# Where four 512 KB loads of the input are issued: SyncE's queue alone, or SyncE's and ScalarE's

## The chip, the cores and the metric

The kernel runs on one core of a Trainium2 chip, with that core's five engines (TensorE or PE, VectorE or DVE, ScalarE or ACT, GpSimd or POOL, SyncE or SP) and its 16 DMA engines. The metric is the device time of one execution in microseconds (us), lower is better, as the median of several runs.

## The reference

Two layers over an input x of 512 positions by 1024 channels, each with an adaLN modulation from a vector c. Cut to what the opening of the kernel works on:

```python
m = silu(c) @ w_mod + b_mod                       # shift, scale, gate
shift, scale, gate = jnp.split(m, 3, axis=-1)
h = rmsnorm(x, norm_g) * (1.0 + scale) + shift    # mean of x*x over 1024 channels
proj = h @ w_in                                   # layer 1: z, bg, cg, xh
y = shortconv_mixer(proj) @ w_out                 # layer 2: spatial gating mixer
x = x + gate * y
```

A final RMSNorm closes it. So nothing of the large products can start before the sum of x*x over all channels and the first columns of shift and scale exist.

## The kernel before

All arrays are transposed: channels on the 128 partitions, positions along the free dimension. x is eight tiles of 128x512 float32, `x_s`, loaded as four quarters of two tiles (512 KB each, 4 KB per partition). The weights come as one stream of slots of 512 KB. Products of full precision are made of three products of float32r, with each operand cut into a high part (ScalarE) and a low part (VectorE).

The opening goes like this. SyncE issues the four quarters of x (L367, semaphores `x_in[0]` to `x_in[3]`), then the stream in the fixed order `START_ORDER`: four slots of the modulation weights for the first channel pair (`raw_s`, "s0", L379), one weight slot (`raw`, L384), four slots "s1", two weight slots, then "s2", which waits until seven additions of the sum of squares are counted (`sq_added >= SQ_START`, with SQ_START 7), and so on. All of them go through one DMA queue, called q1 in the profile. ScalarE issues one load, `cols` (80 KB of constants, 640 bytes per partition, L601), on its own queue, q10; it then waits for it, makes silu(c) (L603) and squares the eight tiles of x in order, each pair after its quarter has landed (L606).

VectorE copies silu(c) into a wide tile `silu_w` (L1507), adds up the squares as they come (`ssum`, seven additions, L1512), takes a part of the modulation product (`acc_s`, L1421 and L1418) and then makes the variance. TensorE's program is in this order: six matmuls that serve only its clock (`keep_clock`, L1003), after the first square; `direct_columns(0, 0)`, 16 matmul instructions on the first slot of s0 (L1050); the column sums of `ssum`, after the seventh addition (L1063); `direct_columns(0, 1)` on the second slot (L1050); the sums of `acc_s` (L1040); the broadcast of the inverse root (L1034); then the first group of s1 (L1050) and the products themselves (L1077, L987 to L989). Engines execute their instructions in order.

The rest of the kernel, from about 54 us on, is two loops of products and two output projections; the changed lines are not in it.

Of the kernel before, what the change touches and what calls it, by code (L numbers as in the profile page):

```python
# [137 lines left out]
def build(nc, stream, xt, cols_d, wst_d, bs_d, out):  # L138
    ctx = ExitStack()
    with ctx:  # L140
# [3 lines left out]
        def sem(name):  # L144
            return ctx.enter_context(nc.semaphore(name))
# [5 lines left out]
        def at_kb(name, kb, shape, dt=F32):  # L151
            return nc.alloc_sbuf_tensor_at(name, shape, dt, offset=base + 1024 * kb)

        x_s = at_kb("x_s", 0, [P, KD, S])
# [84 lines left out]
        cols_in, x_in, ws_in, bs_in = sem("cols_in"), [sem(f"x_in{k}") for k in range(4)], sem("ws_in"), sem("bs_in")  # L239
# [123 lines left out]

        @block.sync
        def _(sp):
            for k in range(4):
                sp.dma_start(x_s[:, 2 * k:2 * k + 2, :], xt[:, 2 * k:2 * k + 2, :]).then_inc(x_in[k], 16)  # L367
            for q, what in enumerate(START_ORDER[:Q_RING]):
                if isinstance(what, str):
# [134 lines left out]
            for n in range(KD):  # L504
                half, k = n // DPAIRS, 2 * (n % DPAIRS)
# [53 lines left out]
        def _(act):  # L559
# [39 lines left out]


            act.dma_start(cols[:, :], cols_d[:, :]).then_inc(cols_in, 16)  # L601
            act.wait_ge(cols_in, 16)
            act.activation(silu_c[:, :], cols[:, C_C:C_C + KD], ACT.Silu).then_inc(sc_ready, 1)  # L603
            for k in range(KD):
# [1611 lines left out]
```

## Time and profile before

| | us |
|---|---|
| median of 3 runs | 821.37 |
| lowest and highest run | 821.09, 823.55 |
| the profiled execution, whole time | 824.04 |
| span of the profiled execution | 821.8 |

The page lists, for the profiled execution, the busy time of each engine, the span cut into 40 slices, the DMA queues, and the chain of work that ended last, followed back from the last instruction: at each step it goes to what released that step. A piece of that chain is time that sets the end; work that is not on it has slack. Between the span and the whole time of the profiled execution lie 2.24 us.

### The profile page before, as it was taken

The page shows a single profiled execution, that of the slowest core. Times are in us where ns is not written, and L with a number is a line of the kernel's source. Part 1 is how long each engine was busy: PE and PEld are TensorE (multiplying, and loading weights), DVE is VectorE, ACT ScalarE, POOL GpSimd, SP SyncE. Part 2 cuts the span into 40 slices and gives each one's busy share as a digit, 9 for nine tenths or more (in the row PEclk, how much of TensorE's full clock was granted, in tenths as well). Part 3 has the DMA queues.
Part 4 walks back from the last instruction along what each step waited for, and adds up shares of the span by engine and source line. Part 5 has one row for each costly group of instructions (what it writes and reads, how often), then busy time and mean ns, then how long its engine had stood idle before and what let it go on. Part 6 is the DMA issues. An engine that isn't in the chain of part 4 may idle for free.

```text
span 821.8 us, 15171 instructions
## 1 busy us (share of the span) xinstructions
PE 804.2 (98%) x5590; PEld 752.4 (92%) x5590; DVE 645.6 (79%) x942; ACT 438.5 (53%) x616; POOL 50.7 (6%) x64
## 2 busy tenths in 40 slices
PE   6999999999999999999999999999999999999996
PEld 6778999999999999987889888899999999988896
DVE  4989999999999999898553786657888888896534
ACT  3576665656656566553222854445676777752220
POOL 1010000000000000000000000010000000000000
PEclk9999999999999999999999999999999999999999
DMA  9885475656666656577421262405554454487103
GB/s 350 345 206 154 154 198 170 195 172 186 179 179 179 186 171 198 169 280 304 161 91 52 78 234 98 129 29 150 154 153 128 134 147 144 137 303 261 52 1 103
DMA packets 39501, 137.84 MB, mean 168 GB/s; under 512 B 4272, under 2 KB 6448, under 8 KB 39472
## 3 DMA queue, kind: packets, MB, share of 16 engines
q1 hardware_dynamic: 32128, 111.16, 36.9%
q0 software_dynamic: 6912, 25.17, 16.3%
q10 hardware_dynamic: 432, 1.13, 0.4%
q8 instruction: 17, 0.28, 0.1%
q14 instruction: 12, 0.10, 0.0%
HBM read 108.09 MB, written 4.19 MB: 137 GB/s over the span
## 4 chain that ended last, share of the span: by engine, by line
PE 93%; DVE 4%; DMA 1%; issue 1%; ACT 1%; SPq 0%; DVEq 0%; ACTq 0%
PE pp L1122 11%; PE pp L1123 11%; PE pp L1124 11%; PE pp L987 8%; PE pp L988 8%; PE pp L989 8%; PE p_aux L1122 7%; PE p_aux L1124 7%; PE p_aux L1123 7%; PE pp L1258 4%; PE pp L1259 4%; PE pp L1260 4%; PE p_aux L1332 2%; DVE acc_s L1418 1%; PE pp L1077 1%; DMA raw_s<-in_stream 1%
## 5 line engine op out<-in xcount | busy, mean ns | idle before, releaser
L1122 PE MATMUL pp<-h_hi,wh 128*128 128x256 f32 x280 | 79.3, 283 | 0.0
L1124 PE MATMUL pp<-h_hi,wl 128*128 128x256 f32 x280 | 79.2, 283 | 0.0
L1123 PE MATMUL pp<-h_lo,wh 128*128 128x256 f32 x280 | 79.2, 283 | 0.0
L1623 DVE TENSOR_TENSOR wl<-wt,wh 128x1024 fp32r<-128x1024 f32 x56 | 66.5, 1217 | 0.2 <-ACT wh L660 0.2
L660 ACT ACTIVATE wh<-wt 128x1024 fp32r<-128x1024 f32 x56 | 58.9, 1054 | 13.6 <-DVE wt L1604 7.6
L571 ACT ACTIVATE w_hi<-raw 128x1024 fp32r<-128x1024 f32 x29 | 30.6, 1058 | 61.8 <-PE pp L989 29.0
L1122 PE MATMUL pp<-s_hi,wh 128*128 128x256 f32 x224 | 63.4, 283 | 0.0
L1123 PE MATMUL pp<-s_lo,wh 128*128 128x256 f32 x224 | 63.4, 283 | 0.0
L1124 PE MATMUL p_aux<-s_hi,wl 128*128 128x256 f32 x224 | 63.4, 283 | 0.0
L1124 PE MATMUL pp<-s_hi,wl 128*128 128x256 f32 x224 | 63.4, 283 | 0.0
L1123 PE MATMUL p_aux<-s_lo,wh 128*128 128x256 f32 x224 | 63.4, 283 | 0.0
L1122 PE MATMUL p_aux<-s_hi,wh 128*128 128x256 f32 x224 | 63.4, 283 | 0.0
L987 PE MATMUL pp<-y_hi,w_hi 128*128 128x512 f32 (+1 forms) x160 | 58.5, 365 | 0.7 <-DVE y_lo L1684 0.4
L1397 DVE TENSOR_TENSOR w_lo<-raw,w_hi 128x1024 fp32r<-128x1024 f32 x32 | 38.9, 1222 | 22.8 <-ACT w_hi L571 22.3
L987 PE MATMUL pp<-y_hi,w_hi_b 128*128 128x512 f32 (+1 forms) x160 | 56.4, 353 | 0.0
L988 PE MATMUL pp<-y_lo,w_hi 128*128 128x512 f32 (+1 forms) x160 | 55.6, 348 | 0.0
L989 PE MATMUL pp<-y_hi,w_lo 128*128 128x512 f32 (+1 forms) x160 | 55.6, 347 | 0.0
L988 PE MATMUL pp<-y_lo,w_hi_b 128*128 128x512 f32 (+1 forms) x160 | 55.5, 347 | 0.0
L989 PE MATMUL pp<-y_hi,w_lo_b 128*128 128x512 f32 (+1 forms) x160 | 55.5, 347 | 0.0
L1122 PEld LDWEIGHTS pp<-h_hi,wh 128*128 128x128 f32 x280 | 53.7, 192 | 0.4 <-issue 0.4
L1123 PEld LDWEIGHTS pp<-h_lo,wh 128*128 128x128 f32 x280 | 53.8, 192 | 0.0
L1124 PEld LDWEIGHTS pp<-h_hi,wl 128*128 128x128 f32 x280 | 53.8, 192 | 0.0
(223 smaller groups left out, 2591.8 us busy)
## 6 DMA issues: line engine op xcount, KB each, us to landing
raw<-in_stream SPq DMA_DIRECT2D x144, 512.0 KB, 4.0
wl<-raw POOLq DMA_DIRECT2D x28, 512.0 KB, 4.5
raw_l<-in_stream SPq DMA_DIRECT2D x18, 512.0 KB, 5.5
raw_s<-in_stream SPq DMA_DIRECT2D x16, 512.0 KB, 13.3
wl_b<-raw POOLq DMA_DIRECT2D x16, 512.0 KB, 4.5
raw_m<-in_stream SPq DMA_DIRECT2D x14, 512.0 KB, 3.2
x_s<-in_xt SPq DMA_DIRECT2D x4, 512.0 KB, 6.0
w_lo_s<-raw POOLq DMA_DIRECT2D x4, 512.0 KB, 5.4
```

Of the source, the lines that this page charges most:

```text
L660: act.activation(wh[g % 2][:, at], wt[g % 2][:, at], ACT.Copy).then_inc(t_hi_cut, 1)
L987: pe.matmul(out, hi, rhs_hi(kt), start=first and n == 0, stop=False)
L988: pe.matmul(out, hi, rhs_lo(kt), start=False, stop=False)
L989: mm = pe.matmul(out, lo, rhs_hi(kt), start=False, stop=last and n == len(kts) - 1)
L1122: pe.matmul(out, hi, hi_of(k), start=fresh and k == 0, stop=False, skip_group_check=not fresh)
L1123: pe.matmul(out, hi, lo_of(k), start=False, stop=False, skip_group_check=not fresh)
L1124: mm = pe.matmul(out, lo, hi_of(k), start=False, stop=k == 3, skip_group_check=not fresh)
L1258: pe.matmul(v_bank(st)[:, :], left_hi, right_hi, start=kt == 0, stop=False)
L1259: pe.matmul(v_bank(st)[:, :], left_hi, right_lo, start=False, stop=False)
L1260: return pe.matmul(v_bank(st)[:, :], left_lo, right_hi, start=False, stop=kt == KD - 1)
L1397: dve.tensor_tensor(lo[:, slot[0], :], raw[:, slot[1], :], f32(hi[:, slot[0], :]), ALU.subtract).then_inc(consumed, 1)
L1623: dve.tensor_tensor(wl[par][:, part], wt[par][:, part], f32(wh[par][:, part]), ALU.subtract).then_inc(t_cut, 1)
```

## The change

Of the four quarters of x, SyncE issues only the first and the third. ScalarE issues the second and the fourth, right behind its load of the constants and ahead of its wait for them. The semaphores, the destinations and everything else stay as they are.

```diff
         @block.sync
         def _(sp):
-            for k in range(4):
+            for k in (0, 2):
                 sp.dma_start(x_s[:, 2 * k:2 * k + 2, :], xt[:, 2 * k:2 * k + 2, :]).then_inc(x_in[k], 16)
@@
             act.dma_start(cols[:, :], cols_d[:, :]).then_inc(cols_in, 16)
+            for k in (1, 3):
+                act.dma_start(x_s[:, 2 * k:2 * k + 2, :], xt[:, 2 * k:2 * k + 2, :]).then_inc(x_in[k], 16)
             act.wait_ge(cols_in, 16)
```

## Rows read from the trace of the kernel before

**Rows 1.** The page: busy time, and the chain that ended last, by engine.

```profile
PE 804.2 (98%) x5590; PEld 752.4 (92%) x5590; DVE 645.6 (79%) x942; ACT 438.5 (53%) x616; POOL 50.7 (6%) x64
PE 93%; DVE 4%; DMA 1%; issue 1%; ACT 1%; SPq 0%; DVEq 0%; ACTq 0%
```

**Rows 2.** The chain in order of time, first 30 us: start us, us, what.

```profile
0.75 0.39 SPq L367
...
2.13 0.50 SPq L367
...
2.67 8.07 DMA raw_s<-in_stream
10.74 0.14 issue
10.88 3.74 PE p_aux L1050 x16
14.62 1.51 PE p_aux L1063 x8
16.13 3.61 PE p_aux L1050 x16
19.74 1.13 PE p_aux L1040 x8
```

**Rows 3.** Waits of engines for DMAs, first 60 us: us in total, times, longest.

```profile
ACT silu_c L603 <- DMA cols<-in_cols: 2.9, 1, 2.9
PE p_aux L1050 <- DMA raw_s<-in_stream: 1.6, 1, 1.6
```

**Rows 4.** DMA issues, us to landing: quarters 1 to 4, then the first slot.

```profile
x_s<-in_xt SPq DMA_DIRECT2D x1, 512.0 KB, 4.6
...
x_s<-in_xt SPq DMA_DIRECT2D x1, 512.0 KB, 5.5
...
x_s<-in_xt SPq DMA_DIRECT2D x1, 512.0 KB, 6.5
...
x_s<-in_xt SPq DMA_DIRECT2D x1, 512.0 KB, 7.3
...
raw_s<-in_stream SPq DMA_DIRECT2D x1, 512.0 KB, 8.1
```

**Rows 5.** DMA queues (packets, MB, share) in 1.8:3.2, 3.2:4.2, 4.2:5.0, 5.0:6.0 us.

```profile
q1 hardware_dynamic: 70, 0.29, 74.2%
...
q1 hardware_dynamic: 45, 0.18, 69.3%
q10 hardware_dynamic: 28, 0.02, 11.4%
...
q1 hardware_dynamic: 74, 0.25, 79.1%
q10 hardware_dynamic: 110, 0.06, 25.0%
...
q1 hardware_dynamic: 110, 0.41, 100.8%
q10 hardware_dynamic: 6, 0.00, 0.9%
```

**Rows 6.** Timeline, 0.8 to 16.2 us: start us, us, engine, line, what.

```profile
0.88 0.39 ACTq L601 DMA_DIRECT2D cols<-in_cols  x1
5.63 2.24 ACT L606 ACTIVATE x_sq<-x_s 128x512 f32<-128x512 f32 x4
6.39 2.90 PE L1003 MATMUL pp<-ones 128*128 128x128 f32 x12 [6.39 <-ACT x_sq L606]
7.60 4.67 DVE L1512 TENSOR_TENSOR ssum<-ssum,x_sq 128x512 f32<-128x512 f32 x6
14.41 1.72 PE L1063 MATMUL p_aux<-ones,ssum 128*128 128x1 f32 x8
```

**Rows 7.** L1050 alone: us, PE busy (x), PEld busy (x), clock, DMA share, GB/s.

```profile
10.88:14.62 3.74, 3.74 (x16) 3.46 (x16) 1.00 1.03 417
15.99:19.60 3.61, 3.60 (x16) 3.47 (x16) 1.00 1.03 411
21.68:23.60 1.92, 1.92 (x16) 1.75 (x15) 1.00 1.03 410
```

## The prediction

> **What bounds the kernel now.** I read the page first. PE is busy for 98% of the span and makes up 93% of the chain that ended last [rows 1], so a change of the opening can only move the start of that chain, and what it moves there arrives at the end once. The chain in order of time says where it starts [rows 2]: SP issues the four quarters of x one behind the other (four pieces, 0.39 to 0.50 us each), then the first slot s0 of the modulation weights at 2.67 us; 8.07 us later, at 10.74, it has landed, and from 10.88 on the pieces are PE's L1050, L1063, L1050, L1040. No other load is on the chain; the waits of the first 60 us agree, with 1.6 us of PE at L1050 for `raw_s`, and 2.9 us of ACT for `cols` that lie beside it [rows 3]. So the number to forecast is the start of the first L1050, now 10.88, and then whether L1063, now at 14.41, can still follow it without a gap. L1063 waits for the seventh addition of squares, so the landing of every quarter of x stands behind it.
>
> Landing times are the issue times plus the durations to landing [rows 2, 4]: the quarters, issued at 0.75, 1.20, 1.66 and 2.13, land at 5.35, 6.70, 8.16 and 9.43, s0 at 10.77. They come 1.3 to 1.5 us apart: a queue in which the bytes ahead, not the issue, set the time.
>
> **The change, part by part.**
>
> *SP loses two issues.* In time order those are 0.42 and 0.50 us with small gaps, so s0 is issued at 2.67 - 1.0, about 1.7 us. But it sat 8.07 us from issue to landing, with four quarters ahead of it. In 5.0 to 6.0 us the DMA engines are fully busy, 110 packets of q1 in 1 us at 0.41 MB [rows 5]; a block of 512 KB is 128 pieces of 4 KB and 16 that signal, 144 packets, 1.31 us. Between issue and service a waiting block gains nothing from being issued earlier. I take 0 for it; the other end is the whole 1.0 us.
>
> *The Trainium skill on this.* The rule speaks against the change: "DMA: Bandwidth & Descriptors", section "Issuing engines are not separate DMA queues", says that loads started from several engines run on the same 16 DMA engines and interleave, and only the sequencer's time of issue is saved. By that rule alone the gain is 0 where the queue is backed up, and 1.0 us by the reading in which the issue pieces of the chain count; the DMA share of 100.8% from 5.0 us on agrees with the first.
>
> *ACT gains two issues.* Its one issue takes 0.39 us at 0.88 [rows 6]. Two more of 0.39 to 0.50 us end at about 2.2 us. Behind them are ACT's table load (1.28 us at 1.30 before, so until about 3.5) and the wait for `cols`, which lands at 5.5 after 2.9 us of idle ACT. That idle time hides the two issues; without it they would cost up to 1.0 us before every square.
>
> *The order in which the bytes arrive.* This is the part that counts. Before the change q1 serves quarter 1, 2, 3, 4, s0. After it, q1 has quarter 1, quarter 3, s0, and q10 has `cols`, quarter 2, quarter 4. How the two share is to be read where both had work. q10, issued at 0.88, has no packet before 3.2 us; 28 of its 144 lie in 3.2 to 4.2, 110 in 4.2 to 5.0, 6 later. q1 has 70, 45, 74 in those stretches, 189 by 5.0: quarter 1 and 45 packets of the next block [rows 5]. So up to 5.0 us I leave everything as it was: quarter 1 lands at 5.35, `cols` at 5.5, silu and the first squares stand at 5.52 and 5.63. From 5.0 on q10 holds quarter 2. The nearest rows show q10 taking at least a packet for each of q1 (110 to 74, though small ones), so I take equal turns, 55 packets per us each.
>
> With that, q1 has 99 packets of quarter 3 left, 1.8 us, to 6.8; then s0, 144 at 55, 2.62 us, to 9.42. Before, s0's last packet was at 5.0 + 99/110 + 3 x 1.31 = 9.83 and it landed at 10.77, 0.94 later. After: 9.42 + 0.94 = 10.36, 0.4 us earlier. q10 has quarter 2 until 5.0 + 2.62 = 7.62 and quarter 4 until 10.24. With 0.80 from last packet to landing (quarter 2 before: 5.90 to 6.70) and 0.94, they land at 8.4 and 11.2, against 6.70 and 9.43. Quarter 3 lands at 7.6 against 8.16. The x that is needed is complete 1.8 us later than before, and s0 comes 0.4 us sooner because q10 started late.
>
> *Does the sum of squares still hide?* A square takes 0.56 us (2.24 for four), an addition comes every 0.8 us (six in 4.67, the last 0.69 long) [rows 6]. Quarter 2 at 8.4: square done at 9.0, then the remaining six additions, 4.67 us: the seventh ends at 13.7. Quarter 4 at 11.2: two squares to 12.35, so the last addition isn't held by it. Before, the seventh ended at 12.27 and L1063 started at 14.41. After, PE starts L1050 at 10.5 and comes to L1063 3.5 us later, at 14.0. The sum stays hidden with 0.3 us to spare. Behind the additions VectorE has `acc_s`, two pieces of together 1.3 us, which now end near 15.0; the variance needs L1063's end, near 15.7. Also behind them are SP's loads of s2 (from 12.30 to 13.7); q1 has by then 13 blocks issued, work until past 18 us, so nothing starves.
>
> *Sum.* -0.4 us on the start of the chain, 0 elsewhere: 824.04 - 0.4 = 823.6 for the profiled execution (span 821.4). That execution is 2.7 us above the median 821.37; the same step from the median gives 821.0.
>
> **The rivals.**
>
> *A. The second queue fills the slow start, or the issue was on the path.* From 1.8 to 5.0 us the DMA engines moved 0.79 MB, at 0.41 MB per us it could be 1.31. The shortfall, 0.5 MB or 1.27 us, is what a second queue could fill at most. For it: q1's share is 69 to 79% there. Against it: q10 shows no packet until 3.2, and `cols` goes ahead of quarter 2 on it. It would bring s0 to about 9.7, still after the clock matmuls (to 9.29), and the squares earlier with it. -1.0 us: 820.4.
>
> *B. The quarters on q10 come too late (slower).* If q10 gets one turn in three (37 packets per us), quarter 2 lands at 5.0 + 3.9 + 0.8 = 9.7 and the seventh addition by that ends at 15.0; quarter 4 lands at 5.0 + 7.8 + 0.94 = 13.7, its squares and the last addition end at 15.6. L1063 then starts at 15.65, not 14.41: +1.25 us, 822.6. It decides from the point where the seventh addition ends after 14.0: quarter 2 later than 8.7, or quarter 4 later than 12.1. For it: the margin is only 0.3 us in my own sum, and large packets of q10 beside q1's aren't shown. Against it: the small ones got their turns. The far end, q10 only after all that q1 holds, would be 13 blocks, 17 us, some +9 us; the 144 packets of `cols` that were served while q1 held x speak against it.
>
> *C. PE's pace in the opening moves.* The granted clock reads 1.00 in all three stretches of L1050, yet 16 instructions take 3.74 and 3.61 us in the first two and 1.92 us in the third [rows 7]: the first two are at the pace of the lower level (1.2 GHz), the third at 2.4. Before them PE was idle until 6.39, ran 2.90 us of L1003, idled 1.6 us and was then busy without a gap [rows 6]. If the rise comes before the second L1050, up to 1.7 us is saved (819.7); if it comes after the third, at least 1.7 us is added (823.1). Nothing in the change fixes which. The runs shown, 821.09 to 823.55, spread that far without any change. The skill, "TensorE: Matmul & The Clock Gate", section "Part 1: The HAM clock gate", says the transition varies from run to run; the spread agrees in size, no row shows its cause.
>
> **How the numbers follow.** Forecast, s0 0.2 to 0.6 us earlier and the squares hidden: 0.47. A: 0.15. B: 0.20, of it 0.01 for the far end. C: 0.18, half each way. The likeliest is 821.0. The range reaches from A with a little of C, 819.8, to C's slow end and the highest run shown, 823.4. A measurement of this kernel can tell about 0.3%, 2.5 us, from no change. The forecast, A and B's 1.25 us are all inside it. Faster by more needs A and C together: 0.03. Slower by more needs the slow side of C on top of B, or the far end: 0.05. Same: 0.92.
>
> **What would show it.** In the profile of the changed kernel: x_s issues on SP at 0.75 and 1.20, on ACT near 1.3 and 1.7; quarter 2 landing near 8.4 and quarter 4 near 11.2 while s0 lands near 10.4; ACT waiting before the third and the seventh square; the seventh addition ending near 13.7 and L1063 without idle PE before it. An idle PE before L1063 released by `ssum` shows B. s0 landing before 10.0 shows A. q10's packets per us beside q1's from 5 us on show the turns. I'm also wrong if `cols` lands over 1.6 us later than 5.5: the first two squares, done at 6.8 now, would then hold back the third beyond quarter 2's landing at 8.4.

## The result, and the profile after

The changed kernel is slower: median 825.17 us (822.47 to 827.32, 22 runs) against 821.4 us (820.73 to 825.96, 22 runs), ratio 1.0034 with a 95% interval of 1.0022 to 1.0045. The forecast was 821.0, the range 819.8 to 823.4, and "slower by over 0.3%" had a chance of 0.05.

The 22 runs of the changed kernel lie on three levels: 8 at 822.5 to 823.0, 5 at 823.9 to 825.4, 9 at 826.8 to 827.3. Those of before lie on two and a rest: 13 at 820.7 to 821.7, 8 at 823.2 to 824.3, one at 825.96. So two things need a cause: the quickest runs are 1.4 us slower, and the share and the height of the slower levels grew. A single profile shows neither: the profiled execution of the changed kernel took 824.16 us, that of before 824.04, spans 822.0 and 821.8.

The page of the changed kernel is in its first lines that of before [rows 1]:

```profile
PE 801.7 (98%) x5590; PEld 749.5 (91%) x5590; DVE 645.2 (78%) x942; ACT 439.1 (53%) x616; POOL 51.7 (6%) x64
```

The difference is at the start of the chain in order of time (start us, us, what), answering [rows 2]:

```profile
1.30 8.77 DMA x_s<-in_xt
10.09 0.64 ACT x_sq L608
10.76 0.70 DVE ssum L1514
...
14.74 0.70 DVE ssum L1514
15.48 1.05 PE p_aux L1065 x8
16.54 3.51 PE p_aux L1052 x16
```

The chain no longer begins with the first slot `raw_s` but with a quarter of x that ScalarE issued at 1.30, quarter 2. (Lines of the changed kernel are 2 higher than before: L1065 is L1063, L1052 is L1050, L1514 is L1512.) The timeline shows the same from the engines' side, answering [rows 6]:

```profile
1.30 0.94 ACTq L603 DMA_DIRECT2D x_s<-in_xt  x2
5.66 0.21 ACT L605 ACTIVATE silu_c<-cols 128x8 f32<-128x8 f32 x1 [2.11 <-DMA cols<-in_cols]
10.09 2.19 ACT L608 ACTIVATE x_sq<-x_s 128x512 f32<-128x512 f32 x4 [3.18 <-DMA x_s<-in_xt]
10.76 4.67 DVE L1514 TENSOR_TENSOR ssum<-ssum,x_sq 128x512 f32<-128x512 f32 x6 [3.12 <-ACT x_sq L608]
10.85 2.02 PE L1052 MATMUL p_aux<-silu_w,raw_s 128*128 128x120 f32 x16 [1.41 <-DMA raw_s<-in_stream]
15.48 1.05 PE L1065 MATMUL p_aux<-ones,ssum 128*128 128x1 f32 x8 [2.62 <-DVE ssum L1514]
16.40 3.65 PE L1052 MATMUL p_aux<-silu_w,raw_s 128*128 128x120 f32 x16
21.64 1.94 PE L1052 MATMUL p_aux<-silu_w,raw_s 128*128 128x120 f32 x16
```

ScalarE waits 3.18 us for quarter 2, VectorE 3.12 us for its square, and PE 2.62 us for the seventh addition, at 15.43 instead of 12.27. L1063 starts at 15.48 instead of 14.41. The first slot is hardly moved: the first L1052 starts at 10.85, before at 10.88.

The packets of the two queues in 5.2 to 6.2 us and in 7.2 to 8.2 us (packets, MB, share), answering the last of [rows 5]:

```profile
q1 hardware_dynamic: 55, 0.23, 92.5%
q10 hardware_dynamic: 14, 0.03, 7.5%
...
q10 hardware_dynamic: 54, 0.22, 53.7%
q1 hardware_dynamic: 53, 0.20, 48.0%
```

From 7.2 us on the queues take equal turns, as forecast. In 5.2 to 6.2 us they move together 0.25 MB, where the kernel before moved 0.42, and q10 has hardly begun quarter 2. Over 5.0 to 7.2 us, the stretch in which the forecast has q10 move 121 packets, all of quarter 2, the two are at one turn in three:

```profile
q1 hardware_dynamic: 123, 0.45, 74.7%
q10 hardware_dynamic: 64, 0.20, 22.3%
```

The first 18 of these 64 are still the constants: q10 has 190 packets by 7.2 us, so 126 by 5.0, and the constants are 144. The Trainium skill says, in "DMA: Bandwidth & Descriptors", section "Queues, rings and completion order", that a DMA engine takes turns between the queues for which it has work and changes only at a packet's end; the 54 to 53 from 7.2 us on agree, the 55 to 14 in 5.2 to 6.2 us do not show it, and no run shows why.

### The profile page after: what moved, and what is told of

It reads as the page before. It is cut to its first block, busy times and chain, and to the rows that moved or that the text cites. A ratio compares the mean times of both kernels' runs of the same rounds, so it can differ in the third digit from the quotient of the medians.

```text
span 822.0 us, 15171 instructions
## 1 busy us (share of the span) xinstructions
PE 801.7 (98%) x5590; PEld 749.5 (91%) x5590; DVE 645.2 (78%) x942; ACT 439.1 (53%) x616; POOL 51.7 (6%) x64
## 3 DMA queue, kind: packets, MB, share of 16 engines
q0 software_dynamic: 6912, 25.17, 16.2%
## 4 chain that ended last, share of the span: by engine, by line
PE 93%; DVE 4%; DMA 1%; issue 1%; ACT 1%; DVEq 0%; ACTq 0%
PE pp L1124 11%; PE pp L1125 11%; PE pp L1126 11%; PE pp L989 8%; PE pp L990 8%; PE pp L991 8%; PE p_aux L1124 7%; PE p_aux L1126 7%; PE p_aux L1125 7%; PE pp L1260 4%; PE pp L1261 4%; PE pp L1262 4%; PE p_aux L1334 2%; DVE acc_s L1420 1%; PE pp L1079 1%; DMA x_s<-in_xt 1%
## 5 line engine op out<-in xcount | busy, mean ns | idle before, releaser
L662 ACT ACTIVATE wh<-wt 128x1024 fp32r<-128x1024 f32 x56 | 59.0, 1056 | 13.7 <-DVE wt L1606 7.6
```

What stands on the lines that cost most here:

```text
L662: act.activation(wh[g % 2][:, at], wt[g % 2][:, at], ACT.Copy).then_inc(t_hi_cut, 1)
```

## The experiments

Where no other number is given, each was timed in 12 runs beside 17 or 35 runs of the kernel before. "High" are the runs above 825.6: 9 of 22 in the changed kernel; of before, 1 of 22 beside it, and up to 7 of 35 beside the experiments.

### Is it the late squares? The kernel before, squares delayed

```diff
             for k in range(KD):
                 act.wait_ge(x_in[k // 2], 16)
+                if k == 2:
+                    for j in range(6):
+                        act.activation(hf[:, j, :], x_s[:, 0, :], ACT.Square)
```

> The kernel before, loads untouched, with six extra squares on ScalarE (their outputs are read by nobody) ahead of the third square, so that it starts near 10.2 us, as in the changed kernel (10.09). Theory S (the change costs time only because the sum of squares now ends at 15.43 and holds L1063 back): L1063 starts near 15.5, the time rises like the changed kernel's, by 1.1 to 1.4 us in the fastest runs and 2 to 4 us in the median, with single runs near 827. Theory D (the sharing of the DMA engines costs something beside that, for instance in the slots): only the 1.1 us of L1063 appear, or less, median below 822.8.

Median 824.23, ratio 1.0022 (1.0005 to 1.0039). One run at 822.6, nine at 823.7 to 824.9, two at 826.3 and 826.6. Its timeline (lines 3 higher than before):

```profile
9.87 3.21 ACT L609 ACTIVATE x_sq<-x_s 128x512 f32<-128x512 f32 x6
10.52 4.67 DVE L1515 TENSOR_TENSOR ssum<-ssum,x_sq 128x512 f32<-128x512 f32 x6 [3.09 <-ACT x_sq L609]
15.24 1.05 PE L1066 MATMUL p_aux<-ones,ssum 128*128 128x1 f32 x8 [2.55 <-DVE ssum L1515]
16.16 3.43 PE L1053 MATMUL p_aux<-silu_w,raw_s 128*128 128x120 f32 x16
```

With no load touched, the late sum alone makes the kernel slower, and the picture behind it is that of the changed kernel's profile at 824.16. Theory D is out as the main cause. That the changed kernel has more high runs (9 of 22 to 2 of 12) isn't explained by it, nor is it outside what chance gives.

### Which quarter? One part of the change at a time

Quarter 4 alone from ScalarE:

```diff
-            for k in range(4):
+            for k in (0, 1, 2):
@@
+            for k in (3,):
```

> One part of the change alone: only the fourth quarter of x from ScalarE's queue, the second stays with SyncE. Theory S: quarter 2 lands at 6.7 as before and holds nothing; quarter 4 is served beside quarter 2 and 3 from 5 or 6 us on and lands by 9 to 10, the seventh addition ends near 12.3 to 12.9, L1063 isn't held: the time of before, 821 to 822 median. If any load of x on the second queue costs the time by itself, it comes out at 823 or more.

Median 821.33, ratio 0.9998 (0.9975 to 1.002), two runs high. L1063 starts at 13.16 in its profile, after 0.39 us of waiting. Quarter 4 lands at 9.0; quarter 3 comes behind it, its squares start at 9.37, and the seventh addition ends at 13.1 (I had 12.9 at most).

Quarter 2 alone from ScalarE:

```diff
-            for k in range(4):
+            for k in (0, 2, 3):
@@
+            for k in (1,):
```

> The other part of the change alone: only the second quarter from ScalarE's queue. If quarter 2 is what holds the sum of squares, it lands near 10 us as in the changed kernel, the third square starts there, L1063 starts at 15.3 to 15.5, and the time is that of the changed kernel, fast runs 822.5, median 824 to 825. If it needs both quarters on that queue (a rate problem and not an order problem), quarter 2 lands by 8.7 and the time is 821.5.

Median 824.93, ratio 1.0036 (1.0017 to 1.0056), four runs each near 822.5, 824.8 and 827.3: the changed kernel again. Its third square starts at 10.02. As far as these times tell, the whole cost of the change is that of moving quarter 2. In this profile the first slot is late as well: the first L1052 starts at 11.74, runs at the slow pace and ends when the sum does, so that L1065, at 15.41, is held by both.

### What makes quarter 2 late? Small pieces ahead of it, the queue, or the order

The constants from SyncE, ahead of its quarters:

```diff
+            sp.dma_start(cols[:, :], cols_d[:, :]).then_inc(cols_in, 16)
             for k in (0, 2):
@@
-            act.dma_start(cols[:, :], cols_d[:, :]).then_inc(cols_in, 16)
             for k in (1, 3):
```

> The changed kernel with the constants issued by SyncE ahead of its quarters, so that quarter 2 is first on ScalarE's queue. If the 144 small packets of the constants ahead of it are what makes quarter 2 late (first packet at 5.9 us instead of the 5.0 that I took), it now starts near 3 us and lands at 6 to 7.5; the seventh addition ends by 13.5 and the time is that of before, 821 to 822. If the second queue is slow to start for another reason, quarter 2 lands after 9 and the time stays at 823 to 825.

Median 821.54, ratio 0.999 (0.9976 to 1.0003), and all 12 runs between 820.9 and 822.0: none on a slower level. Quarter 2, now first on its queue, has landed at 5.9 (0.88 + 5.0), quarter 1 only at 7.8; the seventh addition ends at 14.5 (I had 13.5) and L1063 starts at 14.54. With nothing ahead of it the second queue is quick: q10 has 22 packets already in 1.6 to 2.6 us. But now quarter 1 is late, and the clock matmuls with it (from 8.60).

SyncE alone, quarters in the order 1, 3, 2, 4:

```diff
-            for k in range(4):
+            for k in (0, 2, 1, 3):
```

> The kernel before with SyncE issuing the quarters in the order 1, 3, 2, 4, no load on ScalarE's queue but the constants. If reading quarter 3 right behind quarter 1 is what runs at 0.23 to 0.28 MB per us in 5.2 to 6.2 us (seen in all four kernels with quarter 2 on the second queue), the slow stretch appears here too and the first slot lands near 11.5. If it is the second queue, the rate there is 0.41, quarter 2 lands at 8.1, the first slot at 10.7 and the seventh addition ends near 13.4: L1063 isn't held or by under 0.3 us, time 821 to 822.

Median 822.28, ratio 1.0012 (0.9991 to 1.0032): the time alone shows no difference. The rows of 5.2 to 6.2 us, with no quarter on q10, do:

```profile
DMA packets 83, 0.29 MB, mean 286 GB/s; under 512 B 8, under 2 KB 14, under 8 KB 83
q1 hardware_dynamic: 76, 0.28, 89.7%
```

The slow stretch is there without a second queue. The first slot starts PE's work at 11.70, before at 10.88. Part of the slow stretch is a shift: in 2.6 to 3.6 us this kernel moves more than before (0.24 to 0.19 MB), but by 7.2 us it is behind, with 1.46 MB from 1.6 us on against 1.66.

SyncE alone, order 1, 4, 2, 3, a single execution:

```diff
-            for k in range(4):
+            for k in (0, 3, 1, 2):
```

> One look at the loads: SyncE alone, quarters in the order 1, 4, 2, 3. If any quarter but the neighbour behind quarter 1 is slow, the rate in 5.2 to 6.2 us is 0.23 to 0.29 MB per us, as with 1, 3, 2, 4 (0.286). If it is special to quarter 3, the rate is 0.40.

It took 821.15 us. 5.2 to 6.2 us:

```profile
DMA packets 122, 0.44 MB, mean 438 GB/s; under 512 B 15, under 2 KB 15, under 8 KB 122
```

Full rate. So it isn't any jump behind quarter 1.

Two quarters on the second queue, the third and the fourth:

```diff
-            for k in range(4):
+            for k in (0, 1):
@@
+            for k in (2, 3):
```

> As many loads of x on ScalarE's queue as in the changed kernel, but the third and fourth quarter, with the first and second on SyncE's in that order. Order theory (the slow stretch from 5.2 to 6.2 us comes from quarter 3 being read right behind quarter 1 on a queue, with quarter 2 left for later): the rate there is 0.40 MB per us or more, quarters 3 and 4 start at 5.3 us, quarter 3 lands by 8.3 and quarter 4 by 10, the seventh addition ends before 13.2 and the time is that of before, 821.0 to 821.6. If two loads of x on the second queue are the trouble, the rate is 0.23 to 0.28 again and the time 823 to 825.

5.2 to 6.2 us:

```profile
DMA packets 120, 0.41 MB, mean 414 GB/s; under 512 B 8, under 2 KB 21, under 8 KB 120
q1 hardware_dynamic: 85, 0.33, 79.8%
q10 hardware_dynamic: 35, 0.09, 22.0%
```

The rate is full with two quarters on q10. The rest of the expectation missed: quarter 4 landed at 12.0, not by 10, since slots of q1 took every second turn beside it, and L1063 started at 14.25. Median 822.71, ratio 1.0007 (0.9988 to 1.0026), its quickest runs at 821.5.

Together: the rate in 5.2 to 6.2 us was 0.23 to 0.29 MB per us in all nine profiles in which q1 reads quarter 3 right behind quarter 1 and quarter 2 isn't under way yet (the changed kernel three times, its four variants with other matmuls, quarter 2 alone, and the order 1, 3, 2, 4), and 0.40 to 0.44 in all the others. Why this pair is slow, no run shows.

The order isn't the whole delay. Where the rate was full, the first quarter on q10 still came later than the 8.4 us of my sum: at 9.0 with quarter 4 alone, and in the last variant quarter 3's squares start at 9.49, against 10.09 for quarter 2's in the changed kernel. In both, q10 had 35 packets in 5.2 to 6.2 us beside 73 and 85 of q1. An estimate from that: at the full rate the seventh addition, which ends 5.34 us behind the start of the third square (10.09 to 15.43), would end at 14.4 to 14.8 us, still behind the 14.0 at which my sum had PE arrive.

### What are the levels? Two more profiles of the changed kernel, with no edit

> The changed kernel again, for one more profile. Pace theory: the time goes with the length of the slow pace behind L1063. At 822.5 both the second and the third L1050 take 2.0 us or less; at 824 to 825.4 the second takes 3.4 to 3.7 us; at 827 the third takes over 2.5 us too, or L1034 takes 2.0 instead of 1.1.

> As the look before, the same kernel once more: the same reading by the pace theory, for whichever of the three levels this execution falls on.

They fell on the other two levels, 827.05 and 822.74 us. PE's timeline of the run at 822.74:

```profile
10.78 3.74 PE L1052 MATMUL p_aux<-silu_w,raw_s 128*128 128x120 f32 x16 [1.15 <-DMA raw_s<-in_stream]
15.40 1.05 PE L1065 MATMUL p_aux<-ones,ssum 128*128 128x1 f32 x8 [0.89 <-DVE ssum L1514]
16.32 2.02 PE L1052 MATMUL p_aux<-silu_w,raw_s 128*128 128x120 f32 x16
20.09 1.94 PE L1052 MATMUL p_aux<-silu_w,raw_s 128*128 128x120 f32 x16
```

and of the run at 827.05:

```profile
10.67 3.74 PE L1052 MATMUL p_aux<-silu_w,raw_s 128*128 128x120 f32 x16 [0.95 <-DMA raw_s<-in_stream]
15.31 1.87 PE L1065 MATMUL p_aux<-ones,ssum 128*128 128x1 f32 x8 [0.90 <-DVE ssum L1514]
17.04 3.75 PE L1052 MATMUL p_aux<-silu_w,raw_s 128*128 128x120 f32 x16
20.58 1.72 PE L1042 MATMUL p_aux<-ones,acc_s 128*128 128x1 f32 x8
22.16 2.05 PE L1036 MATMUL p_aux<-work,ones 128*128 128x512 f32 x2
24.00 3.02 PE L1052 MATMUL p_aux<-silu_w,raw_s 128*128 128x120 f32 x16
```

L1065 starts at the same time in both. Everything PE does behind it takes nearly twice as long in the second, until its third L1052 is through: 26.86 against 21.86 us for the next matmul, 5.0 us, and 4.3 us at the end. In these profiles the levels are how long PE stays at the pace of 1.2 GHz after the hold. The profiled execution at 824.16 is the middle one: second L1052 at 3.65, third at 1.94.

It got there in another way. The three L1052 of the run at 824.16, by themselves (stretch, us, PE busy, PEld busy, granted clock, DMA share, GB/s):

```profile
10.85:12.87 2.02, 2.01 (x16) 1.83 (x16) 1.00 1.02 418
16.40:19.91 3.51, 3.51 (x16) 3.38 (x16) 0.51 1.02 407
21.64:23.58 1.94, 1.94 (x16) 1.75 (x15) 1.00 1.03 410
```

and the second and third of the run at 827.05:

```profile
17.04:20.79 3.75, 3.74 (x16) 3.46 (x16) 1.00 1.03 410
24.00:27.02 3.02, 3.02 (x16) 2.84 (x15) 1.00 1.03 410
```

At 824.16 PE was quick in its first group and in L1065, and then its granted clock fell to the lower level and rose again. At 827.05 PE was slow from the first L1052 on, with no fall on record. The mean granted clock listed for each run tells the two apart: it is 0.998 or more in all 122 runs of the kernel before that were timed beside the experiments, and in 8 of the 9 high runs of the changed kernel; it is below that in 4 of the 5 of its middle level and in one high run. With the squares delayed and the loads untouched it is below in 8 of 12 runs. So a fall of the clock comes with the late sum; the longest slow pace does not need one.

### Does PE's idle time decide the level?

The hold's gap filled: four clock matmuls between the first L1050 and the wait for the sum.

```diff
             direct_columns(0, 0)
+            keep_clock(4)
             pe.wait_ge(sq_added, SQ_START)
```

> The changed kernel with four more clock matmuls between the first L1050 and the wait for the sum of squares, that is 1 us of PE at the quick pace, 1.9 at the slow one, in a gap of 0.9 to 2.6 us. If the idle gap of PE lets its pace fall (theory C: the runs near 827 are those in which the slow pace lasts longer), the second L1050 takes 1.9 instead of 3.65 us in more runs, and the share of runs near 827 falls: median 822.5 to 824. If the gap has no part in it, the median stays at 825 or rises by up to 0.6 us, because the filler itself delays L1063 when it runs slowly.

Median 823.42, ratio 1.0013 (0.9996 to 1.003); six runs at 822.4 to 823.0, six at 823.8 to 825.1, none high. In 5 of the 12 the listed clock is below 0.998.

The earlier gap filled, nine clock matmuls for six:

```diff
-WARM = (6, 2)
+WARM = (9, 2)
```

> The changed kernel with nine clock matmuls in place of six ahead of the first L1050: at the slow pace (0.48 us each) they fill the idle gap of PE from 9.4 to 10.85 us. The hold of L1063 by the sum of squares stays. If the spread of the changed kernel (822.5 to 827.3) comes from how long PE stays at its slow pace, and the gap decides that, the slow runs go: most runs near 822.5, 1.1 to 1.4 us above the fast runs of before, none at 827. If the spread has another cause, it stays, median 825.

Median 826.83, ratio 1.0044 (1.0022 to 1.0065), 8 of 12 high. That expectation fell. The profile is of a run at 831.67 us, the highest of the 12:

```profile
10.72 3.00 PE L1052 MATMUL p_aux<-silu_w,raw_s 128*128 128x120 f32 x16
15.68 1.42 PE L1065 MATMUL p_aux<-ones,ssum 128*128 128x1 f32 x8 [1.95 <-DVE ssum L1514]
16.95 3.75 PE L1052 MATMUL p_aux<-silu_w,raw_s 128*128 128x120 f32 x16
```

PE gets through its first group sooner than in the runs at 822.74 and 827.05 and then idles longer in the hold, 1.95 us to 0.9. Behind it the granted clock is 0.50 until about 26 us, and in 11 of the 12 runs the listed clock is below 0.998. This one execution has a second fall far outside the opening, to 0.50 in 378 to 384 us, so its whole time says nothing about the two gaps.

Both gaps filled:

```diff
-WARM = (6, 2)
+WARM = (9, 2)
@@
             direct_columns(0, 0)
+            keep_clock(6)
             pe.wait_ge(sq_added, SQ_START)
```

> The changed kernel with both idle gaps of PE filled: nine clock matmuls ahead of the first L1050, six more (1.5 us quick, 2.9 us slow) between it and the wait for the sum of squares. Nine alone had made it worse (median 826.8): the first L1050 then ran quicker, the idle time before L1063 stayed at 1.95 us, and the pace was slow behind it until about 26 us. If that second gap is what sends the pace down, the runs above 825.5 go and the median is 822.5 to 824.5. If the number of clock matmuls as such is the trouble, it stays near 826.8 or gets worse.

Median 823.89, ratio 1.0017 (1.0001 to 1.0033), none high. With the hold filled, 0 of 24 runs are high in two kernels; without, 9 of 22 and 8 of 12. But the filled hold doesn't keep the clock up: 7 of these 12 runs list less than 0.998, and in the profile, of a run at 825.20, the clock falls behind the hold (second L1052 at 2.79 us with a granted clock of 0.69, third at 2.84 with 0.67). Four runs lie at 825.2 to 825.5, close below the line that I drew for high. What the filler takes away is the highest level, not the slow pace.

The second L1050 moved into the hold:

```diff
             direct_columns(0, 0)
+            direct_columns(0, 1)
             pe.wait_ge(sq_added, SQ_START)
@@
             mm.then_inc(stat_sum, 1)
-            direct_columns(0, 1)
```

> The changed kernel with the second L1050 moved ahead of the wait for the sum of squares: no work added, but PE has work in the time in which it waited. The sum of squares is as late as before the move, L1063 starts near 15.5 (later by up to 2.5 us where both L1050 run at the slow pace). Hold-and-pace theory: median 822.3 to 823.8, the runs above 825.5 are gone or rare, since the hold is filled. If the DMA sharing costs something of its own after 16 us, the time stays at 825.

Median 824.13, ratio 1.0028 (1.0009 to 1.0048), 4 of 12 high: "rare" didn't come. The move opens another gap, 1.71 us before L1042, in its profile. In 9 of the 12 the listed clock is below 0.998. That fits the pace theory but doesn't show it; this run is against the simple form of the theory, that filling the hold is enough.

The same on the kernel before. Nine clock matmuls at once:

```diff
-WARM = (6, 2)
+WARM = (9, 2)
```

> The kernel before with the same nine clock matmuls, loads untouched. Pace theory: its slower runs (823.2 to 826.8, about 4 in 10) go, all near 821.1, the time of the constants-on-SyncE variant, whose clock matmuls happened to run up to the first L1050 and whose 12 runs lay between 820.9 and 822.0. Otherwise the spread stays; and if the three matmuls delay the first L1050, up to 0.2 us is added.

Median 821.05, ratio 0.9986 (0.9964 to 1.0007), 10 of 12 runs at 822.6 or below, two at 824.3 and 826.1.

Nine, each behind a square:

```diff
-            pe.wait_ge(sq_ready, 1)
-            keep_clock(WARM[0])
+            for n, many in enumerate((2, 2, 1, 1, 1, 1, 1)):
+                pe.wait_ge(sq_ready, n + 1)
+                keep_clock(many)
```

> The kernel before, its clock matmuls spread: two behind each of the first two squares, one behind each of the next five, nine in all, so that PE is never idle long before the first L1050 at either pace. Pace theory: first L1050 group at 2.0 to 3.7 us, the slow runs (823 and more) become rarer than before's 4 in 10, median 821.0 to 821.3. The floor of the fast runs, 820.5 to 821, stays, since there the weight slot that lands at 37.2 us and the transfer behind it set the chain.

Median 821.23, ratio 0.9986 (0.997 to 1.0002). Ten runs at 820.4 to 822.5; two were over 1100 us, as one of the kernel before beside them was, and say nothing.

22 from the start, with no wait for the first square:

```diff
-WARM = (6, 2)
+WARM = (22, 2)
@@
-            pe.wait_ge(sq_ready, 1)
             keep_clock(WARM[0])
```

> The kernel before with 22 clock matmuls that don't wait for the first square but only for the constants of GpSimd, so PE runs from about 1.7 us on: 22 x 0.24 to 0.48 us. If the pace at the first L1050 is set by what PE did before, both first L1050 groups take 2.0 us in every run and the time is 820.8 to 821.3 throughout. If it rises too late in the string (all 22 at the slow pace end at 12.3), up to 1.5 us is lost in those runs. If the pace has nothing to do with it, the spread stays as before.

Median 822.69, ratio 1.0014 (0.9993 to 1.0034). Both L1050 groups were at 2.02 us in the profile, as expected, but the time wasn't 821: five runs are at 824.9 to 825.8, and the profiled one is at 822.3, with the transfer of `w_lo_s` on its chain at 8.84 us where the quarter-4 variant below has 7.55. What made the five slow, no profile shows, but all five list a granted clock below 0.998 (0.990 to 0.997), as three of the other seven do and none of the 35 runs of before beside them: in this kernel the clock fell without any hold by the squares. None of the three is a clear gain over the kernel before.

### Why the quickest runs lose 1.4 us and not more

In the profile of the quarter-4 variant (821.18 us), the first two L1052 run at the quick pace, L1065 starts at 13.16, and the chain in order of time goes on thus:

```profile
19.52 1.15 DVE w_lo_s L1399
20.69 16.54 DMA raw<-in_stream
37.25 1.06 ACT w_hi_s L571
38.30 0.96 ACT w_lo_s L577
39.57 7.55 DMA w_lo_s<-raw
...
51.11 5.65 PE pp L1079 x24
```

A load of a weight slot and the transfer behind it take over as the bound. The same last piece starts at 52.43 in the changed kernel's run at 822.74, 1.3 us later, 53.99 in the profiled ones of both kernels (824.04 and 824.16), and 56.87 in the run at 827.05. L1065 starts 2.2 us later than in the quarter-4 variant (15.40 to 13.16); of that the floor of the loads swallows 0.9. The variant with the constants on SyncE agrees: its L1063 at 14.54 goes with 821.46 us.

## Why the prediction was wrong

**Right.** Issue time gave nothing by itself: SyncE issued the slot 1.0 us earlier, PE's first L1050 moved by 0.03 us (I had 0.4). ScalarE's two issues were hidden: its table load ended at 3.55 and it still idled 2.11 us. Equal turns of the queues held from 7.2 us on, not before. The place to look was right: the seventh addition against L1063.

**The term that failed** is "From 5.0 on q10 holds quarter 2 ... I take equal turns, 55 packets per us each". q10 had 14 packets in 5.2 to 6.2 us and 40 in 6.2 to 7.2, and both queues together ran at 0.25 and 0.33 MB per us, not 0.41. By 7.2 us 46 packets of quarter 2 had been moved where the sum had 121. The 75 that were missing, by an estimate from the rows of 5.0 to 7.2 us: 18 because the constants were not through at 5.0, 27 because both queues together had 187 packets and not 242, and 30 because q10 had 64 of these 187 and not half. Quarter 2 landed at 10.1, not 8.4; quarter 4 at 12.6, not 11.2; the seventh addition ended at 15.43, not 13.7. The margin of 0.3 us that the sum left was far smaller than that miss. I had left "up to 5.0 us everything as it was" and the rate behind it as it was, though the order in which q1 reads x changed; the run in the order 1, 3, 2, 4 shows that this order alone slows the stretch. Why q10 gets less than half at first, also where the rate is full, stays open.

**Rival B** is what happened in its effect, and half in its reason: L1063 at 15.48 (B had 15.65), and the quickest runs 1.4 us slower (B had 1.25). Its one turn in three is what 5.0 to 7.2 us show (64 of 187 packets), on top of the lower rate; from 7.2 us on it wasn't one in three but one in two. That B's numbers came out so near is in part luck: it had quarter 2 at 9.7 and quarter 4 at 13.7, and they landed at 10.1 and 12.6.

**Rival C and the chances.** "Nothing in the change fixes which", I wrote of PE's pace, and "slower by more needs the slow side of C on top of B: 0.05". I treated as independent two cases that aren't. B makes PE wait ahead of L1063, and the pace behind the wait is what C is about. With the hold, 14 of 22 runs are on the upper two levels, the highest 4.8 us above the lowest. That the hold brings falls of the clock, and with them the middle level, is shown by the delayed squares (8 of 12 runs with a clock below 0.998, 11 of 12 above 823; before, none of 122 and about 4 in 10). That it also brings the highest level isn't shown: the delayed squares have 2 of 12 runs there and the kernel before, beside them, 5 of 35, though a filled hold has 0 of 24. Which run falls on which level, why the clock also fell in the variant with 22 early clock matmuls and not in the one with two quarters on q10, which holds PE for 1.93 us, and why the moved L1050 didn't help, stays open.

**The base.** I made the sum against an execution in which both first L1050 were slow. Most runs of before lie 2.7 us below it. The profiles of its variants with other clock matmuls, in which PE was at the quick pace by the end of its first L1050, have L1063 at 12.54 to 13.35: there the slack behind the sum of squares, which ended at 12.27 before, is 0.3 to 1.1 us, not 2.1. C's 819.7 has the same fault: it takes the 1.7 us of a slow second L1050 from the median, but a run at 821.15 (order 1, 4, 2, 3) has its second L1050 at 2.02 us already.

## What to carry to other kernels

When a load moves to another queue, work out when each piece lands in its new order, not only when it is issued: equal turns delay whatever was ahead in the old queue, and its consumer may be a chain of other engines. Don't take a queue to be at its full share from the moment at which it could be. Treat a margin of a few tenths of a us in such a sum as no margin, and price its loss together with what an idle PE brings behind it, not as a case apart. If the profiled run lies well above the median, find out what differs in the others before taking slack from it; here that took three profiles of the same kernel.

## What the runs showed of the hardware

- The order of reading matters in the first microseconds: quarter 3 read right behind quarter 1 ran at 0.286 MB per us in 5.2 to 6.2 us on one queue, quarter 4 behind quarter 1 at 0.438. Pieces are 4 KB with 16 KB from row to row in all of them. The cause is open.
- In every profile here 1.6 to 3.6 us ran at 0.15 to 0.28 MB per us, whichever queues were used, against 0.40 to 0.43 from 7.2 us on.
- The granted clock read 1.00 in stretches in which the same 16 instructions took 3.74 and 1.92 us [rows 7], but 0.51 in one in which they took 3.51 (the run at 824.16): here it showed a pace that fell from the quick one, and not one that was slow from the start. The pace of TensorE is to be read from the durations. The Trainium skill, "TensorE: Matmul & The Clock Gate", section "HAM oscillation — how this bites in real kernels", describes PE idling between bursts and starting the next one at the half clock; the run at 824.16 agrees in part, with its first group at 2.02 us, 2.62 us of idle PE, and its second group at 3.65, but the first instructions behind the idle time, L1065, still ran at the quick pace (1.05 us, where the run at 827.05 has 1.87).
